# Three pieces of a head's work put on ScalarE and GpSimd instead of VectorE

## The reference

```python
o_f, s_f = direction(zf, lb_f, s0_f, False)      # hgrn2 scan: S_t = diag(f_t) S_{t-1} + k_t v_t^T, o_t = S_t^T q_t
o_b, s_b = direction(zb, lb_b, s0_b, True)
g, sb, sc, sh, ga, gb = split(h @ w_in[:, REC_COLS:])
o = o_f + o_b
o = o * rsqrt(mean(o * o, axis=-1) + EPS) * a_norm_g
y_a = o * silu(g)
y_b = sb * short_conv_1d(sc * sh, sconv_w)
merged = sigmoid(ga) * (y_a @ w_pa) + sigmoid(gb) * (y_b @ w_pb)
```

## Time and profile before

| | |
|---|---|
| median of 3 runs | 2397.47 us (2397.31 to 2401.25) |
| the profiled execution | 2397.65 us, span in the trace 2396.0 us |
| busy over the span | PE 97%, DVE 68%, ACT 41%, POOL 1% |
| the scan (heads 0 to 7) | from about 439 to 692 us of the span |
| one looped head | 31.7 us |

### The profile page before, as it was taken

How to read it: one execution, slowest core, us unless ns; L and a number is a source line. 1 busy time by engine, 2 the same in 40 slices (tenths; PEclk the granted TensorE clock), 3 DMA queues, 4 the chain that set the end, 5 groups by cost and what they waited for, 6 DMA issues and landing times.

```text
span 2396.0 us, 48924 instructions
## 1 busy us (share of the span) xinstructions
PE 2313.3 (97%) x18474; PEld 2230.2 (93%) x18474; DVE 1639.5 (68%) x2546; ACT 978.7 (41%) x1354; POOL 17.0 (1%) x34
## 2 busy tenths in 40 slices
PE   5699999999999999989999999999999999999999
PEld 3588888999999999989999999999999999999999
DVE  3456565899986666878877888765455676666763
ACT  3322222544434343345444444444344544444442
POOL 0000000000000000000000000000000000000000
PEclk7799999999999999999999999999999999999999
DMA  9955555433357667884555545555555444444453
GB/s 401 372 209 202 218 197 223 160 137 125 140 179 260 229 254 269 326 325 158 182 187 186 180 175 182 188 194 166 177 174 184 170 144 172 141 156 157 143 186 109
DMA packets 67972, 475.58 MB, mean 198 GB/s; under 512 B 7728, under 2 KB 7728, under 8 KB 16848
## 3 DMA queue, kind: packets, MB, share of 16 engines
q1 hardware_dynamic: 66384, 465.50, 53.0%
q0 software_dynamic: 1536, 9.36, 1.1%
HBM read 469.58 MB, written 5.24 MB: 198 GB/s over the span
## 4 chain that ended last, share of the span: by engine, by line
PE 84%; DVE 8%; DMA 3%; issue 3%; ACT 1%; DVEq 0%; SPq 0%; ACTq 0%; POOL 0%; POOLq 0%
PE acc L727 80%; PE aux L727 4%; DMA raw<-wts 3%; DVE lo L1077 2%; DVE ar L1288 2%; DVE sc L1260 1%; DVE qla L1281 1%; DVE tt L1286 1%; PE aux L973 0%; ACT hi L442 0%; DVE yab L1093 0%; DVE hx L1094 0%; ACT n L598 0%; DVE n L1406 0%; DVE qlb L1281 0%
## 5 line engine op out<-in xcount | busy, mean ns | idle before, releaser
L727 PE MATMUL acc<-hx,hi 128*128 128x256 f32 (+1 forms) x5888 | 1172.0, 298 | 15.8 <-DVE hx L1094 8.6
L727 PEld LDWEIGHTS acc<-hx,hi 128*128 128x128 f32 x5888 | 943.5, 192 | 47.7 <-issue 8.6
L1077 DVE TENSOR_TENSOR lo<-raw,hi 128x1024 fp32r<-128x1024 f32 (+1 forms) x720 | 816.0, 1167 | 216.1 <-ACT hi L442 212.1
L727 PE MATMUL acc<-hx,lo 128*128 128x256 f32 (+1 forms) x2944 | 874.9, 297 | 0.0
L442 ACT ACTIVATE hi<-raw 128x1024 fp32r<-128x1024 f32 (+1 forms) x720 | 699.4, 1010 | 381.4 <-PE acc L727 327.0
L727 PEld LDWEIGHTS acc<-hx,lo 128*128 128x128 f32 x2944 | 563.9, 192 | 15.3
L727 PE MATMUL acc<-u,hi 128*128 128x272 f32 (+1 forms) x2048 | 384.1, 288 | 2.8 <-DVE xf L1497 2.8
L727 PEld LDWEIGHTS acc<-u,hi 128*128 128x128 f32 x2048 | 318.5, 188 | 7.5 <-DVE xf L1497 3.0
L727 PE MATMUL acc<-u,lo 128*128 128x256 f32 (+1 forms) x1024 | 291.5, 285 | 0.0
L727 PE MATMUL acc<-sh,hi 128*128 128x256 f32 x704 | 202.4, 288 | 0.4 <-DVE lo L1077 0.4
L727 PE MATMUL acc<-sh,lo 128*128 128x256 f32 x704 | 199.3, 283 | 0.0
(11 more groups left out here) (284 smaller groups left out, 2074.9 us busy)
## 6 DMA issues: line engine op xcount, KB each, us to landing
raw<-wts SPq DMA_DIRECT2D x392, 1024.0 KB, 4.8
raw<-wdown SPq DMA_DIRECT2D x64, 704.0 KB, 4.1
xc<-xct SPq DMA_DIRECT2D x1, 4096.0 KB, 12.5
x<-xct SPq DMA_DIRECT2D x1, 2048.0 KB, 9.8
park<-x POOLq DMA_DIRECT2D x1, 2048.0 KB, 8.8
xf<-park POOLq DMA_DIRECT2D x1, 2048.0 KB, 9.1
outt<-outs POOLq DMA_DIRECT2D x16, 128.0 KB, 2.0
crow_all<-crow SPq DMA_DIRECT2D x1, 1024.0 KB, 23.7
```

What stands on the lines that cost most here:

```text
L727: return pe.matmul(*a, **k)
L1077: V.tensor_tensor(LO[:, slot, a:b, :], RAW[:, p % 4, a:b, :], HI[:, slot, a:b, :].bitcast(F32), ALU.subtract).then_inc(lo_half, 1)
```

## The change

Three pieces of each head leave VectorE.

- The scaling of the normed outputs into `on` (two instructions) is done by ScalarE right behind the power -1/2, with the scale as a per-partition factor. ScalarE's small copy of the factors (L528) and the semaphore `o_rstd` go.
- The copy of the second product into `scb` is done by ScalarE, between the `hi` of unit 3 and the `hi` of the next head's unit 0. It waits for the product, for the bank before it to be given back (VectorE's `gs`, L1316) and, through `yb_ready`, for the last reader of `scb` of the head before.
- The `lo` of unit 3, the fourth of each head, is made by GpSimd in two halves, behind its fill of ones. It waits until VectorE has made the `lo` of unit 2 (`lo_half` is counted in order), and for each half of `hi`. VectorE waits for it before it makes the `lo` of the next unit.

```diff
         def _(pool):
+            def low_half(i):
+
+                s, slot = prod_index("mix", i, 3) - ROWS1, prod_index("mix", 0, 3) % 2
+                pool.wait_ge(lo_half, used("mix", i, 3))
+                for h, (a, b) in enumerate(halves("mix")):
+                    pool.wait_ge(hi_half, 2 * s + h + 1)
+                    nc.gpsimd.tensor_tensor(LO[:, slot, a:b, :], RAW[:, 3, a:b, :], HI[:, slot, a:b, :].bitcast(F32),
+                                            ALU.subtract).then_inc(lo_half, 1)
...
                 nc.gpsimd.memset(AR[:, 1:4:2, :], 1.0).then_inc(hd_ones, 1)
+                low_half(i)
...
                 ch.link(A.activation(SMALL[:, 8:10], SMALL[:, 6:8], ACT.Exp, scale=-0.5))
-                A.activation(SMALL[:, 10:12], SMALL[:, 8:10], ACT.Copy).then_inc(o_rstd, 1)
+                for t in range(2):
+                    ins = A.activation(ON[:, t, :], AUX[:, 3, t * P:(t + 1) * P], ACT.Copy, scale=SMALL[:, 8 + t:9 + t])
+                ins.then_inc(on_ready, 1)
...
                 hi("mix", i, 3)
+                done("mix", i, 1)
+                act.wait_ge(bank_free, prod_index("mix", i, 1))
+                act.wait_ge(yb_ready, 1 + i)
+                A.activation(SCB[:], ACC[:, 1, 0:T], ACT.Copy).then_inc(bank_free, 1)
                 hi("mix", i, 4)
...
-            def mix_on(i):
-
-                dve.wait_ge(o_rstd, i + 1)
-                mark(V.tensor_scalar(ON[:, 0, :], AUX[:, 3, 0:P], SMALL[:, 10:11], None, ALU.mult))
-                V.tensor_scalar(ON[:, 1, :], AUX[:, 3, P:T], SMALL[:, 11:12], None, ALU.mult).then_inc(on_ready, 1)
...
                 level(2)
-                if not peeled:
-                    mix_on(i - 1)
                 level(3)
                 tile_copy(i, 2)
-                lo("mix", i, 3)
...
                 V.tensor_tensor(GS[:], ACC[:, 0, 0:T], SGG[:], ALU.mult).then_inc(bank_free, 1)
-                done("mix", i, 1)
-                V.tensor_copy(SCB[:], ACC[:, 1, 0:T]).then_inc(bank_free, 1)
                 tile_copy(i, 3)
...
                 level(5)
+                dve.wait_ge(lo_half, used("mix", i, 4))
                 lo("mix", i, 4)
...
                 done("mix", i, 2)
+                dve.wait_ge(bank_free, prod_index("mix", i, 2))
                 V.tensor_tensor(UP[:, 1:T + 1], ACC[:, 2, 0:T], SCB[:], ALU.mult).then_inc(bank_free, 1)
...
                     if first:
-                        mix_on(HEADS - 1)
                         mix_ya(HEADS - 1)
```

More of the change, by code:

```diff
@@ L82 @@
 NC2 = _o
-CHAIN = {"v_rec": 7, "v_mix": 22, "v_merge": 4, "v_up": 16, "v_attn": 22, "a_mix": 3, "a_attn": 4}
+CHAIN = {"v_rec": 7, "v_mix": 21, "v_merge": 4, "v_up": 16, "v_attn": 22, "a_mix": 3, "a_attn": 4}
 class Chain:
@@ L278, in build @@
             sem(n) for n in ("hd_init", "hd_ones", "ql_ready", "ks_ready", "qs_ready", "tile_mm", "tile_read"))
-        o_mm, o_rstd, on_ready, on_tr, ya_ready = (sem(n) for n in ("o_mm", "o_rstd", "on_ready", "on_tr", "ya_ready"))
+        o_mm, on_ready, on_tr, ya_ready = (sem(n) for n in ("o_mm", "on_ready", "on_tr", "ya_ready"))
         yb_ready, mrg_ready = sem("yb_ready"), sem("mrg_ready")
@@ L395, in _ @@
             pool.dma_start(park[:, 0:KD // 2, :].rearrange("p k t -> p (k t)"), CROW[:]).then_inc(crow_out, 16)
+            def low_half(i):
[5 more added lines that the diff above has]
+                                            ALU.subtract).then_inc(lo_half, 1)
             pool.wait_ge(bank_free, PROD0["mix"])
             nc.gpsimd.memset(AR[:, 1:4:2, :], 1.0).then_inc(hd_ones, 1)
+            low_half(0)
             with pool.Fori(1, ITERS["mix"]) as i:
@@ L899, in merge_columns @@
                         mix_turn(HEADS - 1, True)
-                        pe.wait_ge(yb_ready, HEADS)
+                        pe.wait_ge(yb_ready, 1 + HEADS)
                     prod("merge", i, p + 2, lambda k: YAB[:, 2 - 2 * (k // 8), k % 8, :], lambda k: YAB[:, 3 - 2 * (k // 8), k % 8, :],
@@ L1062, in _ @@
             V = nc.vector
-            for one in (vt_ready, ya_ready, s_hidden, mix_ready, sq3f_done):
+            for one in (vt_ready, ya_ready, yb_ready, s_hidden, mix_ready, sq3f_done):
                 dve.sem_inc(one, 1)
```

## The result

The changed kernel takes 2407.69 us (median of 8 runs, 2406.46 to 2410.2) where the kernel before, on the same chip, takes 2398.09 (8 runs, 2397.28 to 2401.25): 9.6 us more, ratio 1.0037 with a 95% interval from 1.0026 to 1.0048. It is slower, and by more than the 0.2%, 4.8 us, that the prediction takes as the least that can be told from no change. The profiled execution of after took 2410.2 us, its span is 2408.1, 12.1 more than before's 2396.0.

What follows compares the result with a forecast made beforehand. VectorE was taken to bound a head at 31.69 us. GpSimd's exclusion costs 3.5 us against 3.12 spared, 0.36 a head worse, 2.9 over eight heads: 2397.65 + 2.9 = 2400.5 us, range 2376 to 2408.

Steps and rivals of the forecast that it cites:

- The likeliest case: In the scan, two-operand GpSimd and VectorE instructions exclude each other, d from 1.9 to 2.6: 2400.5 us, chance 0.50.
- side by side: Rival: GpSimd and VectorE run together at no cost, TensorE binds at 29.3 us a head: 2378.5 us, chance 0.32.
- What bounds: In the scan, VectorE bounds a head at 31.69 us; TensorE is next, so no head goes below 29.3 us.
- ScalarE's part at nothing: Scalings of `on` and copy to `scb` on ScalarE: under 1.2 us added, costed at nothing; 0.4 a head without cover.
- The exclusion: Two-operand GpSimd instructions and VectorE ones with two SBUF operands exclude each other: 3.5 us a head against 3.12 spared.
- one subtraction, d: Time of one GpSimd subtraction, half of unit 3's `lo`: taken as 2.2 us.
- first half, on `ql`: VectorE's loss at level 2's `ql` from GpSimd's first half: d - 0.7 = 1.5 us, the rest under tile copies.
- second half, on the next row: VectorE's loss in levels 2 and 3: d = 2.2, or 1.25 if GpSimd starts only at a tile copy; 2.0 taken.
- Between these ends I take the middle, 2.2 us: GpSimd subtraction time, chosen between 1.14 us from VectorE's pace and 3.15 us from three passes at the fill's pace.
- 8 x 0.36: Net loss of 0.36 us a head times eight heads of the scan: 2.9 us.
- The long subtraction: Rival: same exclusion with d near 3.15, 1.5 to 2.5 us a head lost: 2410 to 2417, say 2413; chance 0.11.
- own range: Range of the exclusion case with d from 1.9 to 2.6, -10 to +11 us: given as 2390 to 2408.

Runs made afterwards that it cites:

- the last tile copy: Kernel with only ScalarE's two pieces moved, plus each head's last tile copy moved from VectorE to ScalarE: 2389.76 us, ratio 0.9962.
- the fill: Changed kernel with GpSimd writing zeros into unit 3's low halves, reading nothing, in place of the subtraction: 2381.33 us, ratio 0.9923.
- the run with the copy: Changed kernel with GpSimd copying the two halves of raw unit 3 into the low part, one operand read, instead of subtracting: 2385.1 us, ratio 0.9944.
- the piece of 256 elements: Changed kernel with GpSimd making only 256 of unit 3's 2048 low elements and VectorE the rest in two instructions: 2391.47 us, ratio 0.9965.

## Why the prediction was right, and where it was off

The likeliest case was the one that came, and the time lies in the range. Its value, +2.9 us, was within what counts as no change; the result, +9.6, is beyond it. So the mechanism was right and its sizes were too small, each by little. That the range holds the time owes something to luck: it ends 0.3 us above it, and it is wide enough to take in the opposite mechanism, side by side.

*What bounds.* VectorE bounds the scan, as said: taking work off it makes a head shorter (0.72 us for 0.85, 1.11 for 1.19 with the last tile copy's 0.34), down to TensorE's floor, 29.02 us with the fill.

*ScalarE's part at nothing.* Nearly right: nobody waits for what ScalarE was given, and the run with it alone gains, but the small gap between `ar` and level 3's `ql`, 0.12 us a head, comes with it and had been put at nothing. `gs` ends at 560.09, and the `hi` at 560.46 and the next `lo` at 563.25 don't wait. TensorE's 1.43 us ahead of `on` went. The estimate of ScalarE's new work, "under 1.2 us", does not come out of its own terms (0.26, 0.26 and 0.33 taken three times over are 2.55); by the page it was (984.4 - 978.7) / 8 = 0.71 us a head, and nothing hung on it.

*The exclusion.* That it would come, and not side by side, was the author's estimate: GpSimd reads nothing in the scan of before, and no run had shown the two answers apart. The mechanism was right, and so was its place: the level's `ql` behind the tile copies and one more level-2 row of over 2 us. The terms, as forecast and as measured in a middle head:

| term | forecast, us | measured, us |
|---|---|---|
| one subtraction, d | 2.2 | 2.38 |
| first half, on `ql` | 1.5 | 1.60 (2.27 - 0.68) |
| second half, on the next row | 2.0 | 2.18 (2.43 - 0.25) |
| small gap at level 3 | 0 | 0.12 (556.40 - 555.68 = 0.72 against 0.60) |
| spared | 3.12 | not measured by itself |
| a head, net | +0.36 | +0.77 (3.78 + 0.12 - 3.12 = 0.78) |

The step that was mis-sized is "Between these ends I take the middle, 2.2 us", and it enters twice; with d = 2.38 the same sum gives 1.68 + 2.18 - 3.12 = +0.74. The second half costs d less 0.2, as the forecast's 2.0 was 2.2 less 0.2: of the two cases that the prediction weighed there, the one it leaned to came, since GpSimd began as soon as `hi` was ready, with no tile copy beside it. The cover of the first half was 0.78 us, not 0.7, and the small gap makes up the rest.

*"8 x 0.36".* The heads are not alike. Head 1 lost 2.09 us: nothing of the first half lay under the tile copies (0.50), and VectorE waited for TensorE (0.85). The forecast read one middle head and multiplied it. With head 0 at 1.25, head 1 at 2.09 and six heads at about 0.78 the scan loses 8.0 us, not 2.9. Another 1.6 us of the total lie outside the scan and stay open.

*Who waits for whom.* Where VectorE was the later of the two, it waited for all of the other: `ql` does its own 0.54 us only behind GpSimd's first row. Where GpSimd is the later it waits as well, but its row grows by about 0.15 us less than it overlaps: by 0.11 for 0.26 in after, by 0.26 for 0.40 in the run with the copy. That the fill does not contend is a run of this case (0.25 and 0.69 us beside 0.96), as is that a VectorE copy with its data in PSUM does not (1.02 us for the pair in before and in after).

*The rivals.* "Side by side" fell, and the fill shows its size: 17.5 us, 19.5 in the scan, where 19.1 were worked out. Its floor of 29.3 us a head was close (29.02 measured). The last 0.28 lie in TensorE's rows behind a wait, which the sum took at full pace: in before, four small matmuls right behind one take 0.71 us and the next row starts 0.47 later (551.64 to 552.11), against 0.61 and 0.37 where nothing was waited for (548.14 to 548.51). The long subtraction fell at 2.38 us, though its price, 2413, is a little nearer the result than the forecast's. The forecast's "own range", 2390 to 2408, is narrower than its -10 to +11 us give, 2388 to 2409. What the prediction didn't have at all is that the two parts of the change depend on each other: it priced ScalarE's part at nothing and GpSimd's at 3.5, as if the second alone would cost 8 x (3.5 - 2.27) = 9.8 us; alone it costs 32.4.

## What to carry to other kernels

An engine that excludes the bounding one is no spare engine: price an instruction moved to it by its whole length there, less what lies beside instructions that it doesn't hold, and compare that with what the bounding engine saves (here 4.76 less 0.98 for 2.27 of work moved). The cover that showed here, tile copies with their data in PSUM, has to be there in every iteration, and of the subtractions given to GpSimd only the piece of 256 elements, which fitted under it whole, held nobody (`ql` kept its 0.68 us). Work given to ScalarE, whose `hi` rows keep their 1.06 us beside VectorE's, was worth nearly all that it took off VectorE (0.72 us a head for 0.85), and more where it took a value out of a queue for which TensorE was waiting.

## What the runs showed of the hardware

- A held instruction is not idle in this profile: its row grows (2.27 for 0.68 us, 2.43 for 0.25), and the engine's busy share rises with less work to do. Compare rows of one shape before and after, not busy shares.
- GpSimd took 0.73 us for a two-operand subtraction of 256 elements and 2.38 for 1024, so, as an estimate on a straight line through the two, 2.15 ns an element and 0.18 us fixed; a one-operand copy of 1024 took 1.04, a fill 0.96.
- One operand read by GpSimd held a VectorE instruction with two SBUF operands (1.00 for 0.68 us, 1.04 for 0.20); a fill did not (0.25 and 0.69 us beside 0.96). Tile copies with their mask in SBUF and their data in PSUM were not held (1.02 us for the pair in before and in after).
- With GpSimd's part alone, after 4.75 us of idle time, TensorE ran 5.4 us at a granted clock of 0.53, then at 1.00 again. In after the granted clock stayed at 1.00 across idle times of 1.35 us and, in head 1, of 2.36.
